# Order of high and low products in the mixers' front-weight projections, and a later turn of the compressed keys

## What is computed

```python
def mixer(h, w_in, gate_bias, rpb, w_na_out, w_f_out, w_o):
    z = h @ w_in
    ...
    g_na = jax.nn.sigmoid(ga + gate_bias[0])
    g_f = jax.nn.sigmoid(gf + gate_bias[1])
    return (g_na * y_na + g_f * y_f) @ w_o

def hybrid_mixer(h, w_in, w_gate, ...):
    ...
    g_a, g_b, g_c = jnp.split(jax.nn.sigmoid(h @ w_gate), 3, axis=-1)
    merged = g_a * (o_a @ w_br_a) + g_b * (o_b @ w_br_b) + g_c * (o_c @ w_br_c)
    return merged @ w_out
```

## Time and profile before

| | |
|---|---|
| median of 3 runs | 2235.17 us (2234.65 to 2236.45) |
| the profiled execution, its own time | 2236.18 us |
| its span in the trace | 2234.3 us |
| PE, DVE, ACT busy | 2228.1, 1834.1, 1131.7 us |
| granted TensorE clock, mean | 1.00 |
| mix1 gates in layers one and two, about | 246 to 302 us, 765 to 822 us |
| mix2 gates in layers one and two, about | 1310 to 1409 us, 1898 to 1998 us |

### The profile page before, as it was taken

The page is one execution under the profiler, slowest core; times in us unless marked ns, Lnnn a source line. Parts: engine busy times, 40 slices in busy tenths (PEclk is TensorE's granted clock), DMA queues, the critical chain, the costliest instruction groups (busy, mean ns, idle before and its releaser), DMA issues.

```text
span 2234.3 us, 42466 instructions
## 1 busy us (share of the span) xinstructions
PE 2228.1 (100%) x16140; PEld 2052.3 (92%) x16140; DVE 1834.1 (82%) x3023; ACT 1131.7 (51%) x1503; POOL 4.8 (0%) x10
## 2 busy tenths in 40 slices
PE   9999999999999999999999999999999999999999
PEld 8998999999999999999999889999999998999998
DVE  8888568888888668887988878888898887888887
ACT  5445465445445465444434676654354446766443
POOL 0000000000000000000000000000000000000000
PEclk9999999999999999999999999999999999999999
DMA  7555445555555435654556443555556555344663
GB/s 252 194 194 207 160 153 198 197 196 170 198 197 207 170 133 191 214 192 165 200 190 206 170 152 125 178 196 191 188 178 205 189 172 189 123 141 166 221 196 133
DMA packets 76817, 407.63 MB, mean 182 GB/s; under 512 B 9264, under 2 KB 9920, under 8 KB 44336
## 3 DMA queue, kind: packets, MB, share of 16 engines
q1 hardware_dynamic: 75792, 404.93, 53.2%
q10 hardware_dynamic: 720, 0.89, 0.1%
q0 software_dynamic: 208, 0.49, 0.1%
HBM read 405.23 MB, written 1.05 MB: 182 GB/s over the span
## 4 chain that ended last, share of the span: by engine, by line
PE 97%; DVE 2%; issue 0%; ACT 0%; DVEq 0%; ACTq 0%
PE ps_proj L684 13%; PE ps_aux L693 13%; PE ps_y L263 10%; PE ps_y L264 10%; PE ps_y L265 10%; PE ps_proj L688 7%; PE ps_aux L696 7%; PE ps_proj L1110 4%; PE ps_proj L1117 4%; PE ps_proj L1111 4%; PE ps_proj L263 2%; PE ps_proj L264 1%; PE ps_proj L265 1%; PE ps_aux L651 1%; PE ps_proj L651 1%; PE ps_aux L1931 1%
## 5 line engine op out<-in xcount | busy, mean ns | idle before, releaser
L130 DVE TENSOR_TENSOR w_lo_front<-w_raw_front,w_hi_front 128x2048 fp32r<-128x2048 f32 x238 | 544.1, 2286 | 42.5 <-ACT w_hi_front L105 42.2
L105 ACT CAST w_hi_front<-w_raw_front 128x2048 fp32r<-128x2048 f32 x238 | 452.9, 1903 | 178.6 <-PE ps_aux L696 145.0
L263 PE MATMUL ps_y<-hidden_lo,w_hi_back 128*128 128x256 f32 x1344 | 372.5, 277 | 0.1
L265 PE MATMUL ps_y<-hidden_hi,w_hi_back 128*128 128x256 f32 x1344 | 371.5, 276 | 0.0
L264 PE MATMUL ps_y<-hidden_hi,w_lo_back 128*128 128x256 f32 x1344 | 371.5, 276 | 0.0
L105 ACT CAST w_hi_back<-w_raw_back 128x1024 fp32r<-128x1024 f32 x248 | 259.9, 1048 | 146.8 <-PE ps_y L265 120.1
L877 ACT ACTIVATE silu_gate<-silu_gate 128x256 f32<-128x256 f32 x176 | 73.7, 419 | 508.3 <-DVE silu_gate L914 508.2
L684 PE MATMUL ps_proj<-xt_lo_hi,w_hi_front 128*128 128x512 f32 x1280 | 319.8, 392 | 0.0
L693 PE MATMUL ps_aux<-xt_lo_hi,w_hi_front 128*128 128x512 f32 x1280 | 319.6, 392 | 0.0
L130 DVE TENSOR_TENSOR w_lo_back<-w_raw_back,w_hi_back 128x1024 fp32r<-128x1024 f32 x248 | 302.3, 1219 | 4.0 <-ACT w_hi_back L105 3.3
L684 PEld LDWEIGHTS ps_proj<-xt_lo_hi,w_hi_front 128*128 128x128 f32 x1280 | 228.6, 188 | 39.6
(11 more groups left out here) (462 smaller groups left out, 3828.3 us busy)
## 6 DMA issues: line engine op xcount, KB each, us to landing
w_raw_front<-in_stream SPq DMA_DIRECT2D x251, 1024.0 KB, 4.9
w_raw_back<-in_stream SPq DMA_DIRECT2D x252, 512.0 KB, 3.7
m_rel_bias<-in_rel_bias SPq DMA_DIRECT2D x2, 2048.0 KB, 8.0
m_params<-in_params SPq DMA_DIRECT2D x2, 656.0 KB, 4.7
w_raw_front<-in_stream SPq DMA_DIRECT2D x4, 256.0 KB, 6.9
w_raw_front<-in_stream SPq DMA_DIRECT2D x2, 512.0 KB, 8.7
x<-in_x ACTq DMA_DIRECT2D x3, 256.0 KB, 6.7
out<-x SPq DMA_DIRECT2D x3, 256.0 KB, 2.2
```

The lines of the kernel that those rows point to most:

```text
L105: self.nc.scalar.copy(self.hi[part][:, parity], self.raw[part][:, parity]).then_inc(self.hi_done[part], by)
L130: eng.tensor_tensor(self.lo[part][:, parity], self.raw[part][:, parity], self.hi[part][:, parity].bitcast(F32), ALU.subtract).then_inc(sel ...
L263: nc.tensor.matmul(out, ah, bl, start=start, stop=False)
L265: return nc.tensor.matmul(out, ah, bh, start=False, stop=stop)
```

## The change

In `project`, chunks of the front buffer without `xn` and `between` get another order: the two high products of k = 0, then the eight low products (chunk 0 with its wait for the split ahead of them), then the fourteen high products of k = 1 to 7. In `mix2_tensor` the transpose of the compressed keys moves from ahead of gate 2 to behind it. The number of instructions is the same; DVE's, ACT's and the queues' programs are unchanged.

```diff
@@ project
+    def by_high(k, stop):
+        part = hi[:, k * P:(k + 1) * P]
+        nc.tensor.matmul(out, part, s.nl[:, k], start=k == 0, stop=False)
+        return nc.tensor.matmul(out, part, s.nh[:, k], start=False, stop=stop)
+
+    if c != 2 and xn is None and between is None:
+        by_high(0, False)
+        if c != 1:
+            pe.wait_ge(w.split[0], base + slot + 3)
+        for k in range(KD):
+            nc.tensor.matmul(out, lo[:, k * P:(k + 1) * P], s.nh[:, k], start=False, stop=False)
+        for k in range(1, KD):
+            last = by_high(k, k == KD - 1)
+        w.taken(last, c)
+        return
     for k in range(KD):
         ...
-        part = hi[:, k * P:(k + 1) * P]
-        nc.tensor.matmul(out, part, s.nl[:, k], start=k == 0, stop=False)
-        nc.tensor.matmul(out, part, s.nh[:, k], start=False, stop=False)
+        by_high(k, False)
@@ mix2_tensor
     index(1)
+    gate(2)
     need("kc_dup", 1)
     pe.sem_inc(s.order, 1)
     mark.inc(nc.tensor.transpose(s.pa[1][:, 0:2 * CB], m.kc2[:].rearrange("c e d -> c (e d)"),
                                  s.ident[0:2 * CB, 0:2 * CB]), "kcT_done")
-    gate(2)
```

## The result

| | before | after |
|---|---|---|
| median, us | 2235.55 (2234.65 to 2236.45, 6 runs) | 2244.21 (2244.03 to 2245.34, 6 runs) |
| profiled execution, us | 2236.18 | 2245.34 |
| its span, us | 2234.3 | 2243.5 |
| mean granted clock | 1.00 | 1.00 |

The changed kernel is slower by 0.4%: the ratio is 1.004, with a 95% interval of 1.003 to 1.005. The medians are 8.7 us apart, the two spans 9.2.

What follows compares the result with a forecast made beforehand. PE's order, busy in all of the span, was taken as the path. Pauses of +10.4 us less 0.8 for pace gave +9.6: 2245.8 us for the profiled execution, 2244.8 for the median, range 2239.5 to 2249.5.

Steps and rivals of the forecast that it cites:

- The sum: Whole kernel: +10.4 us of pauses less 0.8 of faster matmuls, +9.6 us; median 2244.8 us, 0.43% slower.
- The wait moved forward: Mix2's chunk 0 at slots 9, 11, 13, 14, 15: PE waits for the split, +10.4 us over both layers.
- d: DVE's delay against the old trace in mix2; near 0 at slot 11 of layer one, 1.6 us at job 8.
- D: PE's delay against the old trace in mix2; 1.6 us behind slot 11, 5.2 behind slot 15, in each layer.
- Handing on: Mix2: PE's delay makes DVE late where DVE waits for PE, so pauses don't simply add; +10.4 us, chance 0.70.
- adding up: Rival: all mix2 pauses add up in full, +13.7 us, 2248.9 us; chance 0.11.
- The transpose: Mix2, behind gate 2: 0.24 us gained less 0.11 cost, 0.13 a layer, swallowed at slot 11.
- the uncovered case: Mix2: if slot 11's wait did not swallow the moved transpose's gain, it would be worth 0.26 us in all.
- The pace of the matmuls: Reordered chunks, mostly mix1: early low run enters the fast pace, 0.06 us a chunk, -0.8 us taken in all.
- catch up: Rival: DVE does not pass on PE's delay, each layer pays its largest shortfall only; +2.6 us, 2237.8 us; chance 0.10.
- faster: Rival: every reordered chunk runs fast from its third matmul and splits come in time; -4.5 us, 2230.7 us; chance 0.03.
- The clock did not fall: Rival: mix2's pauses lower the granted clock, 2.8 us a pause, +28 over ten, 2273 us; chance 0.02.

Runs made afterwards that it cites:

- experiment 2: New order only for mix2's gates on chunk 0 of their slot, transpose at its old place, against the kernel before: 2246.18 us, ratio 1.0048.
- experiment 6: Changed kernel with four high pairs instead of one ahead of the wait in mix2's first chunks: 2238.38 us, ratio 1.0013 to the kernel before.
- experiment 7: Changed kernel with DVE's front split moved ahead of the same step's search round in mix2: 2236.48 us, ratio 1.0005 to the kernel before.
- Experiment 5: Changed kernel with slot 9's chunk 0 (gate 1) of mix2 in the old order again: 2245.64 us, ratio 1.0044 to the kernel before.
- the repeat: Changed kernel with mix2's gate 1 in the old order, run again on one chip with its two-pair sister: 2245.35 us.
- experiment 9: Changed kernel with mix2's gate 1 in the old order and two high pairs ahead of slot 11's wait: 2243.39 us; run again, 2243.95 us.
- experiment 3: Kernel before with only the transpose of the compressed keys moved behind gate 2, all chunks in the old order: 2235.47 us, ratio 1.000.

## Why the prediction was right, step by step

**The sum** was +9.6 us on the profiled execution and 2244.8 for the median. Measured: +9.2 and 2244.21. The verdict and the mechanism held. That the sum is so near is in part luck: mix1's pace alone gave 0.7 us more than the whole pace term, and the feed-forward stretches, which had no part in the sum, came out 0.25 us longer. The errors of the pauses cancel between the layers (below).

**The wait moved forward.** The ten places were right, and so was that slots 10 and 12, gate 22 and mix1 have no pause. The term was +10.4; the trace has 5.44 + 4.99 = 10.43, with the pace of mix2's other chunks and the transpose in it, and experiment 2, which has this part alone, 10.66 in its trace and +10.8 by its median. That it is the place of the wait against the end of the split is shown from both sides, by experiment 6 (wait later, loss smaller) and experiment 7 (split sooner, three quarters of mix2's loss gone).

**The agreement hides errors of size that cancel, which is luck.** At slot 11 of layer one I had put d near 0, because job 3 had "over 1.6 us" of air. The split came 0.42 us late all the same: 1340.87 + 1.15 - 1341.60. The place that I had not looked at is the compressed scores, on which DVE now waits 0.27 us for PE (the row at 1328.37; PE was 1.2 us late there, behind slot 9). DVE is 0.23 late from that row on (it stood at 1329.29 before), and 0.42 from a row at 1331.05; what the last 0.19 waited for I did not resolve. In layer two DVE came to these scores later by itself, and is 0.04 late. So the pause was 1.05 in place of the 0.6 that I had listed, and D 2.01 in place of 1.6. On the other side, from slot 11 to slot 15 the delay grew by 3.51 us in layer one and by 3.45 in layer two, against the forecast 3.6 in both. The three chunks with a pause got longer by 3.78 in layer one and 3.72 in layer two (I had 0.4 for slot 14's pause, and it was 0.62), but the better pace of chunks in between takes 0.27 us off again.

**Handing on against adding up.** Experiment 5 was meant to decide, and its median could not, since the clock came in. Layer one of its two traces can, with the clock at 1.00: without slot 9's pause of 1.2 us mix2 costs 5.03 and 4.95 us in place of 5.44, so 0.4 and 0.5 came back, where handing on gave 0.4 and adding up 1.2. The runs with the clock at 1.000 agree: +8.2, and +8.0 and +8.8 in the repeat, where handing on gave +7.9 and adding up +6.3. The two-pair kernel of experiment 9 (+8.0 and +8.3) also has two matmuls fewer behind the wait and says less about it.

**The transpose.** The gain of 0.24 was right. Its cost at the new place, which I took as 0.11 from the pace of its neighbours, is 0.32: the small transpose now stands between two groups and breaks the pace. In experiment 3's trace it is 0.207 us from gate 2's last matmul to it, 0.173 from it to the next, and 0.165 to the one behind; before, it was 0.117 from gate 2's last matmul to the group and 0.108 to the one behind. My bound of 0.15 from above was too low, and the term has the other sign: 0.08 us lost by gate 3 and not 0.13 gained. It is small beside the pauses, which made this harmless. In the uncovered case the prediction gave 0.26 us of gain for both layers; experiment 3 shows 0.1 of loss in its trace.

**The pace of the matmuls** was -0.8 in all and measures -1.48 in mix1 alone, 0.73 and 0.75 a layer where I had written 0.2 to 0.4. I had said I would be wrong if mix1 moved by more than 1 us: for both layers together it did, and the term was mis-sized by about half. The mechanism, a chunk that comes to the fast pace at the entry to its low run, was as described. The rows of mix1's second query chunk show it: the low run starts at the same 219.26 as the third matmul did before, and ends at the fast pace:

```profile
219.26 1.07 PE L1116 MATMUL ps_proj<-xn_lo_hi,w_lo_front 128*128 128x256 f32 x8
220.17 0.28 PE L1108 MATMUL ps_proj<-xn_lo_hi,w_hi_front 128*128 128x256 f32 x1
```

0.91 us for eight, 0.114 each, where the high run had 0.118. What was too small is the reach. I had counted 0.06 us for each of the 16 chunks of sixty where the pace had changed there. In mix1 alone nine of the sixteen reordered chunks of each layer are shorter, by 0.05 to 0.09 us. This second query chunk is 2.62 us long where it was 2.69; of the later ones, gate 0 falls from 2.81 to 2.73, and the next one, which keeps the old order (`c == 2`), from 2.71 to 2.61. So the fast pace can be carried on into the next chunk. Why some chunks enter it and others don't stays open.

The Trainium skill ("TensorE: Matmul & The Clock Gate", Back-to-back issue gap) lists one gap for an isolated matmul of 256 columns, 262 cycles. Taken as the one pace of these chunks, it would have made the gain 0. The trace disagrees: it has 0.118 and 0.114 us in the same kernel.

**The rivals.** DVE didn't catch up, since its waits for PE grew (0.65 to 1.44 us at job 14). The splits did not come sooner, which the rival "faster" needed. The matmuls behind the wait didn't overtake it: at slot 13 the low run starts at 1368.09 and the next high product at 1369.12. The clock did not fall in the changed kernel, but in one with a pause 0.4 us longer than its longest (1.65). I had given that rival 0.02 with 2.8 us for each pause; where it came, it came once in an execution and cost 1.6 to 2.2 us between the runs of one kernel. It was nearer than I took it to be.

## What to carry to other kernels

Before moving a wait forward on the engine that sets the end, list for each of its places when the thing waited for is ready and when the engine gets there, and keep the other engine's delay in the account as well: it decides whether the next pause is smaller. A wait that is just met has no room, and the work that stands between is its cover. Where the rows show the places with room and those without, make the change only at the first, or move the producer's work first. A pause removed may lengthen the next one, and that one may lower the clock.

## What was not expected of the hardware

Pauses of PE of 2.02 and 2.11 us, after a stretch in which it was busy, were followed by some 3 us at a granted clock of 0.50 (1.2 GHz) in the profiled runs. The runs of the same kernel at a mean clock of 0.999 were 2.2 us (experiment 5) and 1.6 us (its repeat) longer than those at 1.000. Pauses of 1.89, 1.79 and 1.74 us left the clock at 1.00. The step isn't sharp from run to run: with the longer pause seven of ten runs had it, with the shorter one, one of ten, by their mean clock. That the pause's length decides is shown by these two kernels only, which differ by the place of two matmuls; what else takes part stays open. The Trainium skill ("TensorE: Matmul & The Clock Gate", HAM oscillation) tells of kernels whose clock falls behind waits and comes back; the traces of experiment 5 and of its repeat agree.

A single 32x32 transpose between two groups of matmuls cost PE 0.32 us (experiment 3), more than twice what its own 0.15 us to the next start had shown at its old place.

Mix1's stretch of PE, 86.25 us long, came out the same to 0.02 us in every trace with the same order of its matmuls. So a stretch on an engine that waits for nothing there can be compared between traces far more finely than the times of whole runs, which spread by 1 to 2 us.
